# Six instead of four early expert-score tiles between the query tiles of a top-16 stage

## What is computed

```python
q = (hf @ w_q).astype(jnp.float32).reshape(t, PEER_HEADS, 2, PEER_QDIM // 2)
s = jnp.einsum('thsd,hskd->thsk', q, subkeys.astype(jnp.float32))
top_s, top_i = lax.top_k(s, PEER_TOPK)
cand_s = top_s[:, :, 0, :, None] + top_s[:, :, 1, None, :]
cand_i = top_i[:, :, 0, :, None] * PEER_NKEYS + top_i[:, :, 1, None, :]
best_s, best_pos = lax.top_k(cand_s.reshape(t, PEER_HEADS, PEER_TOPK * PEER_TOPK), PEER_TOPK)
...
gate = jax.nn.softmax(best_s, axis=-1)
...
act = jax.nn.gelu(jnp.einsum('thkd,td->thk', ub, hb).astype(jnp.float32))
return jnp.einsum('thk,thkd->td', (gb * act).astype(vb.dtype), vb)
```

## Time and profile before

| | |
|---|---|
| median of 3 runs | 2159.38 us (2158.15 to 2161.4) |
| the profiled execution | 2157.02 us, its span 2155.2 us |
| mean granted clock of TensorE in it | 0.975 of 2.4 GHz |
| PE busy | 2031.6 us, 94% of the span |
| DVE busy | 1591.7 us, 74% |
| ACT busy | 1009.3 us, 47% |
| POOL busy | 263.2 us, 12% |

### The profile page before, as it was taken

One profiled execution on the slowest core, in us unless ns is written; L12 is line 12 of the kernel. 1 busy time (PEld: TensorE's weight loads), 2 busy tenths in 40 slices (PEclk: granted clock), 3 DMA queues, 4 the chain that ended last, 5 costly groups with the idle time before them and its releaser, 6 DMA issues.

```text
span 2155.2 us, 34123 instructions
## 1 busy us (share of the span) xinstructions
PE 2031.6 (94%) x11088; PEld 1745.0 (81%) x11088; DVE 1591.7 (74%) x3434; ACT 1009.3 (47%) x1641; POOL 263.2 (12%) x309
## 2 busy tenths in 40 slices
PE   4898989999999999999969989899999999999997
PEld 3697979888888888788758979798888888888885
DVE  7976889767766768788488858896667766787654
ACT  3223328655555554664341242485555555445543
POOL 1001529400000000000020033590000000000000
PEclk8999989999999999999989999899999999999998
DMA  9458311355555655577365662114555555555561
GB/s 375 152 209 317 113 45 62 115 190 182 193 193 187 214 211 178 180 271 280 121 246 173 248 254 79 50 50 161 194 187 184 194 207 206 191 179 195 186 223 53
DMA packets 115016, 390.57 MB, mean 181 GB/s; under 512 B 12672, under 2 KB 20480, under 8 KB 114432
## 3 DMA queue, kind: packets, MB, share of 16 engines
q1 hardware_dynamic: 114944, 389.64, 51.3%
HBM read 383.82 MB, written 5.77 MB: 181 GB/s over the span
## 4 chain that ended last, share of the span: by engine, by line
PE 64%; DVE 23%; issue 6%; ACT 4%; DVEq 1%; POOL 1%; DMA 1%; SPq 0%; ACTq 0%
PE ps L832 26%; PE ps L823 14%; PE ps L825 6%; PE ps L594 3%; PE ps L720 3%; DVE v_lo L1583 3%; DVE onehot_gate L1562 2%; PE ps L796 2%; PE ps L746 2%; DVE u_lo L1578 2%; DVE w_ada_ring L1289 1%; POOL w_q_lo L919 1%; DVE gated L1591 1%; PE ps L756 1%; ACT gelu L1162 1%
## 5 line engine op out<-in xcount | busy, mean ns | idle before, releaser
L823 PE MATMUL ps<-h_hi_lo,u_hi 128*128 128x512 f32 x1760 | 642.7, 399 | 7.3 <-DVE u_lo L1578 7.3
L825 PE MATMUL ps<-h_hi_lo,u_lo 128*128 128x256 f32 x1540 | 433.4, 281 | 0.0
L823 PEld LDWEIGHTS ps<-h_hi_lo,u_hi 128*128 128x128 f32 x1760 | 332.5, 189 | 77.9 <-issue 6.5
L825 PEld LDWEIGHTS ps<-h_hi_lo,u_lo 128*128 128x128 f32 x1540 | 292.6, 190 | 8.4
L1578 DVE TENSOR_TENSOR u_lo<-weight_ring,u_hi 128x1024 fp32r<-128x1024 f32 x220 | 268.5, 1221 | 17.8 <-ACT u_hi L1151 15.1
L832 PE MATMUL ps<-v_hi,gated_hi 128*128 128x512 f32 x880 | 275.7, 394 | 4.4 <-DVE gated_lo L1597 4.0
L832 PE MATMUL ps<-v_lo,gated_hi 128*128 128x512 f32 x880 | 273.1, 392 | 0.0
L832 PE MATMUL ps<-v_hi,gated_lo 128*128 128x512 f32 x880 | 271.1, 389 | 0.0
L1156 ACT ACTIVATE v_hi<-weight_ring 128x1024 fp32r<-128x1024 f32 x220 | 232.5, 1057 | 76.3 <-PE ps L832 76.3
L1583 DVE TENSOR_TENSOR v_lo<-weight_ring,v_hi 128x1024 fp32r<-128x1024 f32 x220 | 268.0, 1218 | 0.3 <-ACT v_hi L1156 0.3
L1151 ACT ACTIVATE u_hi<-weight_ring 128x1024 fp32r<-128x1024 f32 x220 | 231.7, 1054 | 6.0 <-DMA weight_ring<-in_u_tab_dram 5.5
(11 more groups left out here) (286 smaller groups left out, 3042.0 us busy)
## 6 DMA issues: line engine op xcount, KB each, us to landing
weight_ring<-in_u_tab_dram SPq DMA_DIRECT2D x228, 512.0 KB, 4.4
weight_ring<-in_v_tab_dram SPq DMA_DIRECT2D x220, 512.0 KB, 3.5
w_ada_ring<-in_w_ada_dram SPq DMA_DIRECT2D x80, 512.0 KB, 6.6
weight_ring<-in_w_in_dram SPq DMA_DIRECT2D x46, 512.0 KB, 4.1
v_tail<-in_v_tab_dram SPq DMA_DIRECT2D x36, 512.0 KB, 4.3
weight_ring<-in_w_q_dram SPq DMA_DIRECT2D x32, 512.0 KB, 3.5
u_ahead<-in_u_tab_dram SPq DMA_DIRECT2D x20, 512.0 KB, 8.3
weight_ring<-in_w_out_dram SPq DMA_DIRECT2D x16, 512.0 KB, 4.4
```

Of the source, the lines that this page charges most:

```text
L823: last = mm(both, UH[:, b, k, :], HB[:, :, k, :], start=(k == 0), stop=(k == KT - 1))
L825: mm(PS[:, 4 + b, 0:T], UL[:, b, k, :], HH[:, k, :], start=False, stop=False)
```

## The change

`AHEAD_AT` goes from four entries to six: ahead tiles 0 to 5 stand after query tiles 4, 6, 8, 10, 12 and 14, instead of ahead tiles 0 to 3 after query tiles 5, 8, 11 and 14. Three ahead tiles (6, 7, 8) instead of five (4 to 8) follow the last key scores. On ACT the fixed list behind the loop moves with it.

```diff
-AHEAD_AT = (5, 8, 11, 14)
+AHEAD_AT = (4, 6, 8, 10, 12, 14)
...
                     if n in AHEAD_AT:
                         gelu_ahead(AHEAD_AT.index(n))
-                gelu_ahead(4)
-                gelu_ahead(5)
+                gelu_ahead(6)
+                gelu_ahead(7)
                 act.wait_ge(gate_in, l + 1)
                 fn(GATE[:, :, :], GATE[:, :, :], ACT.Exp).then_inc(gate_exp, 1)
-                for a in range(6, A_TOP):
+                for a in range(8, A_TOP):
                     gelu_ahead(a)
```

## The result

The changed kernel takes **2168.17 us** (median of 8 runs, 2165.56 to 2174.87) against 2159.43 us for the kernel before, timed beside it (8 runs, 2156.16 to 2161.81). The ratio is 1.0044, with 1.0032 to 1.0055 as its 95% interval: some 9 us slower. Forecast were 2170.8 us, a range of 2167.0 to 2175.5, and slower by over 0.2% with 95 in 100. The profiled execution of the changed kernel took 2171.23 us, for a span of 2169.4.

A forecast was written before the change was run, and what follows sets the result against it. PE, not the sorting DVE, was taken to set the pace of the top-16 stage. Two layers x 5.69 = 11.4 us, other terms 0, on a median of 2159.38 gave 2170.8 us, range 2167 to 2175.5.

The forecast's parts named there:

- The loop: Query copy of tile 4 to that of tile 15: 57.22 us instead of 51.53, 5.69 us more per layer.
- The rival of free work: Top-16 stage: DVE sets the pace, ahead tiles fill PE's idle time, time stays at 2159.4 us; 3 in 100.
- A: Stretch from query copy of tile 4 to that of tile 15, forecast at 57.22 us.
- The tail: Behind the last key scores: two ahead tiles fewer, 6.9 us of PE, worth 0; PE idles 8.2 us.
- B: Stretch from query copy of tile 15 to the gates' transposes; removing PE work there was forecast worth 0.
- The rival of a released tail: Behind the last key scores: fewer ahead tiles move selection 6.9 us ahead, -1.2 per layer, 2157.0 us; 2 in 100.
- The clock in selection: From the gates' transposes on: moment of the granted clock's rise, taken as 0, ends -1.9 and +3.2 us per layer.
- C: Stretch from the gates' transposes to the copy of the picked keys, where the clock's effect was taken as 0.
- the case of a clock that stays low: Selection: long PE idle time costs 3.2 us a layer on top, 2177.2 us; 10 in 100.
- The sum: Whole kernel: 2 layers x 5.69 = 11.4 us more, giving 2170.8 us, +0.53%.
- Everything else: ACT's gelus and exponential, the store of the first eight gelus and the ten loads: each worth 0.

The follow-up runs named there:

- the second set: The changed kernel, unedited, timed again beside the kernel before: 2169.22 us against 2160.61, ratio 1.0038.
- the cut tail: Kernel before (four ahead tiles in the loop), but ahead tiles 7 and 8 make only the first of their eight matmuls: 2161.64 us, ratio 1.001.
- the tail filled: Changed kernel, but ahead tiles 7 and 8 make their eight matmuls twice behind the loop: 2166.99 us, ratio 1.0029.
- three in the loop: Kernel before with AHEAD_AT = (5, 9, 14), six ahead tiles behind the last key scores: 2156.76 us, ratio 0.9981; one more run 2157.5 us.
- five in the loop: Kernel before with AHEAD_AT = (4, 6, 8, 11, 14), four ahead tiles behind the last key scores: 2165.57 us, ratio 1.0029.
- one in the loop: Kernel before with AHEAD_AT = (14,), eight ahead tiles behind the last key scores: 2155.8 us, ratio 0.9974.
- two with the low part split: Kernel before with AHEAD_AT = (7, 14) and POOL's subtraction for the low part of w_q split into four instructions: 2151.07 us, ratio 0.9953.
- six early: Kernel before with AHEAD_AT = (3, 4, 5, 6, 7, 8), three ahead tiles behind the last key scores: 2182.65 us, ratio 1.0105.

## Why the prediction was right

**The loop.** Predicted 57.22 us, measured 57.24, in both layers and in three profiles with this `AHEAD_AT`. PE busy throughout, copies at 6.77 and 3.32, no POOL wait, DVE waiting 12.2 / 5 = 2.4 us in each pair: all as forecast. The stretch with three, four, five and six in the loop is 48.05, 51.5, 54.6 and 57.24. This term, +5.7 us a layer, is shown. The times foretold from the start of the span, such as the transposes at 305.7, came 4.4 us later, since the copy of tile 4 did (228.02 against 223.65); counted from it, the first sort of tile 14 and the transposes come 5.7 us later than before, as forecast. The rival of free work falls with it: work beside DVE's sorting is free only where DVE is the one waited for. Inside A that was so in no profile of three or more in the loop; with two PE waited for DVE 2.45 us in one layer and 0.2 in the other, and with one 3.0 and 2.7.

**The tail.** Predicted 0; B is 24.82 before and 24.83 after. It is shown from both sides: 6 us less PE work with the loop of before brought nothing, 6.9 us more with the loop of the change cost nothing. PE idled 8.24 us where 8.2 were forecast. The rival of a released tail falls.

**The clock in selection.** Taken as 0, between -1.9 and +3.2 us a layer. C has a mean of 7.26 us over four pieces of the kernel before and 7.88 over four of the change: +0.6 a layer, within the bounds. The prediction took the piece of a single profile as that of before (7.84 us to the end of the second side, 7.87 by C). It isn't fixed: before, the clock fell in three of the four pieces and once not at all. In the change it had fallen ahead of the picked keys in all four. So in these pieces the long idle time made sure of what had happened in most without it, and the case of a clock that stays low (2177.2 us) didn't come: it rose while ahead tile 9 ran, as before, some 2.5 us behind the start of the transposes in one piece and some 5 in the other three. The second layer had the later rise:

```profile
1380.00:1381.00 1.00, 1.00 (x4) 0.50 0.00 0
1381.00:1382.00 1.00, 1.00 (x6) 1.00 0.00 0
```

**The sum.** Here the size was off, inside the range. The forecast was +11.4 us; measured were 8.7 and, in the second set, 8.6. The stage itself lost more than that: A + B + C over both layers is 167.2 us in the mean of the two profiles of before and 179.9 in the two of the change, +12.7, of which 11.5 is A and 1.2 is C. Outside the stage the profiles give nothing back: the rest of the span is 1987.2 and 1991.5 us in those of before, 1990.0 and 1987.9 in those of the change. The 4 us lie between the profiled executions and the medians. Those of before (2157.02 and 2159.73 us) are 2.4 and 1.4 below the medians beside them, and those of the change (2171.23 and 2170.04) are 3.1 and 0.8 above theirs.

The granted clock goes the same way. It is 0.975 and 0.976 in the profiles of before and 0.972 in both of the change, but 0.9748 against 0.9732 in the mean of the runs of the second set. So the gap between the kernels is 0.0035 in the profiles and 0.0016 in the runs. The difference is some 8 us at 1.2 GHz, worth up to half of it, 4 us: an estimate from these means.

The prediction added the stage's change to the median of before and had no term for this. It was 1.3 us short of what the stage lost in the profiles, and came out 2.6 us above the median. That the median lies inside the range owes something to luck, since the range was made for another piece, the clock in selection.

The part outside the stage moves without any edit. The copy of tile 4 in the first layer, ahead of which the kernels don't differ in order, stands at 223.65 and 226.25 in the two profiles of before and at 228.02 and 227.80 in those of the change, with a mean granted clock of 0.93 and 0.92 against 0.91 and 0.91 over the first 220 us. Another piece is the end: from the last late gelu of the second layer to the end of the span it is 692.34 us in the first profile of before and 688.5 in both of the change. In that first profile the clock was low near the end (two stretches of 5 us, columns as in the earlier trace rows):

```profile
2135.00:2140.00 5.00, 2.62 (x16) 2.26 (x17) 1.09 (x4) 0.54 (x2) 0.00 (x0) 0.74 0.10 27
2140.00:2145.00 5.00, 4.98 (x14) 4.09 (x15) 2.17 (x6) 3.90 (x8) 0.00 (x0) 0.58 0.00 0
```

In the change it was not:

```profile
2154.00:2159.00 5.00, 3.88 (x24) 3.36 (x23) 3.23 (x8) 3.25 (x9) 0.00 (x0) 1.00 0.00 0
```

The other profile of before has 688.4 at its end as well, so this is a matter of the execution at least as much as of the kernel. Of all the profiles only that of the cut tail has 692.4 too, and there the clock was low at the same distance from the end:

```profile
2145.00:2150.00 5.00, 4.10 (x10) 3.33 (x11) 3.05 (x8) 4.44 (x9) 0.00 (x0) 0.50 0.02 3
```

Over the 12 runs of one kernel, too, the time goes with the clock: with the tail filled from 2160.76 us at 0.981 to 2171.16 at 0.975, and with three in the loop as told above.

For the other kernels A + B + C, against the 167.2 of before, agrees with the ratios, inside their intervals, in five cases: five in the loop (+6.2 and +6.3), the cut tail (+1.3 and +2.2), one in the loop (-3.3 and -5.6), two with the low part split (-8.6 and -10.2), and six early (+15.9, and two ahead tiles of 3.4 that lie before A: +22.7, as measured). It doesn't in the change itself and in three more: with the tail filled it gives +11.5 against +6.3, three in the loop (the mean of two profiles) should gain 7.3 us and gained 4.1 (0.9981), and two in the loop should gain 7.2 and gained 13 (0.994, its interval 9 to 17). Which restart of the clock moves in these, and whether the edit moves it, stays open.

**Everything else.** ACT, the loads and the store were taken at 0. The exponential keeps its 10.98 us behind the last copy, and from the copy of the picked keys to the last late gelu it is 96.2 to 96.9 us in the profiles of the change and 96.2 to 96.6 in those of before.

**A faster kernel.** With two ahead tiles in the loop instead of four, at (7, 14), the kernel takes 2148.17 us, 0.6% less than before (0.994, 0.9922 to 0.9957). That the change went the wrong way from four is the plainest outcome of the study.

## What to carry to other kernels

Before work is moved under another engine's, ask which engine is waited for at that very place: filler on the engine that sets the pace costs its whole time (here 3.44 us a tile), and work taken from a stretch where the other engine leads brings nothing back. Count the steps of a loop by kind, with and without the filler, and multiply: that gave the stretch to 0.02 us. A piece that depends on the granted clock should be read in several profiles before it is used as a term, and a sum over a stage is right for the stage only, since the rest of a kernel of 2 ms can move by some us on its own. The mean clock of each run, set beside its time, shows whether a difference may lie there.

## What was not expected of the hardware

DVE's short sums of two operands stand still while POOL runs its subtraction of two operands. A group of four candidate sums (line 1490) takes 0.44 us in the earlier trace rows, but 2.66 us in the kernel with two ahead tiles in the loop. The timeline of DVE there:

```profile
261.81 2.66 DVE L1490 TENSOR_TENSOR candidates<-top_scores 128x32 f32<-128x32 f32 x4
264.51 0.24 DVE L1265 MAX8 best<-candidates 128x8 f32<-128x72 f32 x1
```

That of POOL:

```profile
262.06 2.40 POOL L919 TENSOR_TENSOR w_q_lo<-weight_ring,w_q_hi 128x1024 fp32r<-128x1024 f32 x1 [0.94 <-ACT w_q_hi L975]
```

And PE, which waits for the scores that DVE frees:

```profile
266.75 1.19 PE L734 MATMUL ps<-subkeys_T,query_T 128*128 128x128 f32 x4 [2.45 <-DVE key_scores L1272]
```

POOL starts 0.25 us into DVE's group and ends at 264.46, and DVE's next instruction starts at 264.51. A single sum there, the last of the four, starts 0.03 us behind POOL's instruction and takes 2383 ns, to POOL's end; over that whole profile the median is 169 ns:

```profile
L1490 DVE TENSOR_TENSOR candidates<-top_scores x128: 152/169/2383, 222.1 to 1340.8; 128x16 f32<-128x16 f32 x64, 128x32 f32<-128x32 f32 x32, 128x8 f32<-128x8 f32 x32
```

In the kernel before the longest is 829 ns, and in the change 836: there one sum a layer meets POOL's instruction, and only its last third. In the first layer of before it starts at 219.65 and ends at 220.48, POOL's instruction at 218.04 and 220.43:

```profile
219.65 1.08 DVE L1490 TENSOR_TENSOR candidates<-top_scores 128x32 f32<-128x32 f32 x4
```

```profile
218.04 2.39 POOL L919 TENSOR_TENSOR w_q_lo<-weight_ring,w_q_hi 128x1024 fp32r<-128x1024 f32 x1 [2.27 <-ACT w_q_hi L975]
```

Two in the loop had five groups of about 2.6 us, one in the loop four, three in the loop four (in either profile), six early two. Splitting POOL's instruction in four, with the same `AHEAD_AT`, cut the longest group to 1.39 us and the longest single sum to 745 ns, with pieces of POOL of 0.73 us, which shows that the standstill goes with the length of one POOL instruction. With three in the loop a long group at 259.74 costs DVE 2.2 us, and DVE waits for PE nowhere behind it, so it can account for the 1.1 us that B missed; no run of that kernel had the split. With six early it is about half of the 4.3 us.

The Trainium skill, SBUF — State Buffer, section Who interferes with whom, states that a DVE instruction with two SBUF inputs contends with a GpSimd instruction that reads SBUF. The same page, section SBUF: two separate sides, has it that whichever of the two starts first gets the shared ports for its whole instruction while the other is blocked. The trace agrees: a sum of 0.17 us takes 2.38, 2.2 us of standstill beside 2.40 of POOL's instruction, which itself isn't lengthened. DVE's sorting instructions keep their time beside POOL: in the profile of two in the loop a MAX8 over 128 key scores has a median of 0.28 us with and without it, and a FIND_INDEX8 one of 0.29. That a later sum lost to a POOL instruction that began inside its group fits the rule of who starts first, as each sum is an instruction of its own.
